# Pooling over shifted rows on the vector engine in place of a matrix product, in a two-block transformer kernel

## The reference, cut to what matters

```python
def centred_multiscale_pool(u):          # u (B, L, 4 groups, 512)
    cs = jnp.concatenate([jnp.zeros_like(uf[:, :1]), jnp.cumsum(uf, axis=1)], axis=1)
    left = win // 2                      # win = (2, 4, 8, 16), one for each group
    right = win - 1 - left
    hi = jnp.minimum(t + right + 1, L)
    lo = jnp.maximum(t - left, 0)
    s = cs[:, hi, g] - cs[:, lo, g]
    mean = s / (hi - lo)
    return (mean - uf)

def pool_branch(h, w_in, w_grp, b_grp, scale, w_out):
    u, gate = jnp.split(h @ w_in, 2, axis=-1)
    p = centred_multiscale_pool(u.reshape(B, L, 4, 512))
    p = jnp.einsum('blgc,gcd->blgd', p, w_grp) + b_grp
    y = p.reshape(B, L, 2048) * scale
    return (y * jax.nn.silu(gate)) @ w_out
```

## Time and profile before

| what | us |
|---|---|
| median of 3 runs | 2324.95 |
| lowest, highest | 2322.79, 2325.65 |
| the profiled execution | 2320.34 |
| its span | 2318.5 |
| TensorE busy | 2274.8 (98%) |
| DVE busy | 1677.5 (72%) |
| ACT busy | 1028.1 (44%) |

### The profile page before, as it was taken

How to read it: one execution, slowest core, us unless ns; L and a number is a source line. 1 busy time by engine, 2 the same in 40 slices (tenths; PEclk the granted TensorE clock), 3 DMA queues, 4 the chain that set the end, 5 groups by cost and what they waited for, 6 DMA issues and landing times.

```text
span 2318.5 us, 30884 instructions
## 1 busy us (share of the span) xinstructions
PE 2274.8 (98%) x11041; PEld 1885.8 (81%) x11041; DVE 1677.5 (72%) x2394; ACT 1028.1 (44%) x1474; POOL 77.9 (3%) x113
## 2 busy tenths in 40 slices
PE   8999999999999999999999999999999899999997
PEld 6878888888888888777878888888888799999876
DVE  5479976688788887787879676667874778666644
ACT  5565655555555554344462222222322634544432
POOL 1022200000000000000000000000000000000000
PEclk9999999999999999999999999999999999999999
DMA  8966645667676676787856555555664367422243
GB/s 243 215 185 207 192 137 172 196 215 229 213 238 223 223 228 204 232 264 245 258 169 211 170 180 162 174 156 164 227 200 132 121 188 219 132 74 63 72 158 133
DMA packets 225945, 430.33 MB, mean 186 GB/s; under 512 B 13847, under 2 KB 38671, under 8 KB 224688
## 3 DMA queue, kind: packets, MB, share of 16 engines
q1 hardware_dynamic: 222112, 418.96, 58.1%
q10 hardware_dynamic: 3152, 9.83, 1.3%
q0 software_dynamic: 576, 0.14, 0.0%
HBM read 426.16 MB, written 2.72 MB: 185 GB/s over the span
## 4 chain that ended last, share of the span: by engine, by line
PE 74%; issue 17%; DVE 4%; DMA 3%; ACT 1%; DVEq 0%; POOL 0%; SPq 0%; ACTq 0%; POOLq 0%
PE ps L641 46%; PE ps L676 13%; PE ps L653 10%; DMA raw<-in_w_down 2%; DVE ada_acc L610 1%; DVE lo L579 1%; PE ps L2437 1%; PE ps L2333 1%; PE ps L690 1%; ACT hi L575 1%; DMA xres<-in_x 1%; DMA raw<-in_w_up 0%; PE ps L2197 0%; PE ps L830 0%; DVE ustage L1794 0%
## 5 line engine op out<-in xcount | busy, mean ns | idle before, releaser
L575 ACT ACTIVATE hi<-raw 128x1024 fp32r<-128x1024 f32 x604 | 634.3, 1060 | 943.8 <-PE ps L641 358.1
L579 DVE TENSOR_TENSOR lo<-raw,hi 128x1024 fp32r<-128x1024 f32 x604 | 731.1, 1223 | 396.2 <-ACT hi L575 393.4
L610 DVE SCALAR_TENSOR_TENSOR ada_acc<-raw,csil,ada_acc 128x512 f32<-128x512 f32 x720 | 493.3, 749 | 4.8 <-DMA raw<-in_ada_w 4.6
L641 PE MATMUL ps<-hi,h_hi 128*128 128x512 f32 x960 | 382.1, 398 | 0.4 <-DVE lo L579 0.4
L641 PE MATMUL ps<-hi,h_lo 128*128 128x512 f32 x960 | 378.8, 395 | 0.0
L641 PE MATMUL ps<-lo,h_hi 128*128 128x512 f32 x960 | 378.8, 395 | 0.0
L641 PE MATMUL ps<-hi,g 128*128 128x512 f32 x704 | 227.2, 398 | 9.1 <-DVE lo L579 9.0
L641 PEld LDWEIGHTS ps<-hi,h_hi 128*128 128x128 f32 x960 | 180.8, 188 | 44.2 <-DVE lo L579 3.5
L641 PEld LDWEIGHTS ps<-hi,h_lo 128*128 128x128 f32 x960 | 180.7, 188 | 42.3
L641 PEld LDWEIGHTS ps<-lo,h_hi 128*128 128x128 f32 x960 | 180.9, 188 | 40.7
L641 PEld LDWEIGHTS ps<-hi,g 128*128 128x128 f32 x704 | 132.5, 188 | 44.2 <-DVE lo L579 14.2
(11 more groups left out here) (328 smaller groups left out, 3428.4 us busy)
## 6 DMA issues: line engine op xcount, KB each, us to landing
raw<-in_ada_w SPq DMA_DIRECT2D x192, 512.0 KB, 4.3
raw<-in_w_up SPq DMA_DIRECT2D x176, 512.0 KB, 4.5
raw<-in_w_down SPq DMA_DIRECT2D x88, 512.0 KB, 5.0
raw<-in_w_in SPq DMA_DIRECT2D x84, 512.0 KB, 4.6
raw<-in_pool_w_in SPq DMA_DIRECT2D x64, 512.0 KB, 4.4
raw<-in_mla_w_in SPq DMA_DIRECT2D x56, 448.0 KB, 4.1
raw<-in_w_out SPq DMA_DIRECT2D x32, 512.0 KB, 3.7
raw<-in_pool_w_out SPq DMA_DIRECT2D x32, 512.0 KB, 4.6
```

The lines of the kernel that those rows point to most:

```text
L575: act.activation(hi[:, to, :, :], raw[:, slot, :, :], ACT.Copy).then_inc(hi_split, 1 + ada)
L579: dve.tensor_tensor(lo[:, to, :, :], raw[:, slot, :, :], hi[:, to, :, :].bitcast(F32), ALU.subtract).then_inc(lo_split, 1)
L610: ins = dve.scalar_tensor_tensor(acc, raw[:, slot, k, :], csil[:, v, kt:kt + 1], acc, ALU.mult, ALU.add)
L641: mm = pe.matmul(ps[:, bank, 0:n], tokens(a, kt0 + k, tok), w[:, slot, k, col0:col0 + n], start=first and k == 0 and s == 0, stop=last and ...
```

## The change

What it does, on each engine:

- TensorE: the pooling product is gone. The u panel is made by `by_channels`, so that the weights are stationary and u comes out as channels by tokens. The product with `w_grp` moves from w12, w13 to w14, w15, behind six gate chunks (w8 to w13). w16 and w17 are the last two gate chunks. Both `turn_ada` now stand between w16 and w17. The u panel of groups 1 to 3 gets a wait for the first two silu of the group before (`gate_silu4`).
- ACT: copies u in two halves to `upad`, in which each row of 256 tokens has 8 zeros on either side. Rounds `pt_hi` from `upad`. Evicts the group product to `y` itself, with scale and bias.
- DVE: sums shifted rows (`window_sums`): level 0 adds the row and the row one token back, each further level adds two shifts of the level before, so that window 2^(n+1) takes n+1 additions, for each of two halves. An edge multiply corrects the first and last tokens. Then `upad = sums / window - upad`, and `pt_lo` from it. The eviction of y is gone.
- the banks: in group 0 the u panel is in banks 0, 1, 6, 7 and the gate in 2 to 5, and the norms of the stage ahead move their banks to fit. The first panel's parts for context and latent tokens are 256 columns wide on 24 weight tiles, in place of 512 columns on 12 token tiles.
- ACT no longer loads `poolm` in the w_down stage (four loads of 256 KB), but one small table `edges`.

```diff
+    edges = np.ones((POOL_G, 2, max(POOL_WINDOWS) // 2), np.float64)
...
+        def window_sums(e, n, half):
+            step = sums_done(n, half) - n - 2
+            spans = [(0, SEQ)]
+            for level in range(n, 0, -1):
+                spans.insert(0, (spans[0][0] - 2 ** (level - 1), spans[0][1] + 2 ** (level - 1)))
+            src = upad[:, 2 * half:2 * half + 2, :, :].rearrange("p m s t -> p (m s) t")
...
+            for level, (a, b) in enumerate(spans):
+                to = buffers[level % 2]
+                back, ahead = (1, 0) if level == 0 else (2 ** (level - 1), 2 ** (level - 1))
+                if level:
+                    e.wait_ge(window_summed, step + level)
+                e.tensor_tensor(to[:, :, reach + a:reach + b], src[:, :, reach + a - back:reach + b - back],
+                                src[:, :, reach + a + ahead:reach + b + ahead], ALU.add).then_inc(window_summed, 1)
...
# ACT
-                act.wait_ge(y_gated, FREE + n * 4)
-                act.activation(u[:, :, :], ps[:, 0:4, :], ACT.Copy).then_inc(u_ready, 1)
-                his(act, C_POOL, i, step, ahead(CH), ahead(CH + 2))
                 act.wait_ge(pt_lo_done, FREE + n)
+                for half in (1, 0):
+                    b0 = U_BANKS[n][2 * half]
+                    act.activation(upad[:, 2 * half:2 * half + 2, :, reach:reach + SEQ],
+                                   ps[:, b0:b0 + 2, :].rearrange("p m (s t) -> p m s t", s=2), ACT.Copy).then_inc(u_ready, 1)
+                his(act, C_POOL, i, step, ahead(CH), ahead(CH + 4))
...
+                his(act, C_POOL, i, step, ahead(CH + 4), ahead(CH + 8))
+                act.wait_ge(chunks_used, done(CH + 7))
+                for m in range(4):
+                    ins = act.activation(y[:, n * 4 + m, :], ps[:, U_BANKS[n][m], :], ACT.Identity,
+                                         scale=col(V_POOL_S, n * 4 + m), bias=col(V_POOL_B, n * 4 + m))
+                ins.then_inc(grouped, 1)
                 if n == POOL_G - 1:
...
+                    his(act, C_POOL, i, step, ahead(CH + 8), ahead(CH + 9))
                     for k in range(Y_FIRST):
                         y_high(k)
# DVE
-                split(place_of(0) + RING, place_of(CH + 2) + RING)
+                split(place_of(0) + RING, place_of(CH) + RING)
+                dve.wait_ge(u_ready, 2 * n + 2)
+                sums = itertools.chain(window_sums(dve, n, 0), window_sums(dve, n, 1))
+                for k in range(3):
+                    for _ in itertools.islice(sums, -(-2 * (n + 2) // 3)):
+                        pass
+                    split(place_of(CH + k) + RING, place_of(CH + k + 1) + RING)
...
-                ins.then_inc(grouped, 1)
# TensorE
+                    pe.wait_ge(gate_silu4, (n - 1) * 4 + 2)
+                    for j in range(CH):
+                        by_channels(pe, i * step + at, split_slot(at), h4_hi, h4_lo, CK_T * j, U_BANKS[n], j == 0, j == CH - 1, ada_behind(at))
...
-                            mm = pe.matmul(ps[:, m, s * SEQ + c0:(s + 1) * SEQ], u[:, TT * (1 - s) + k, m * P:(m + 1) * P],
-                                           poolm[:, bass.ds(n, 1), k, c0:].rearrange("p a b -> p (a b)"),
...
+                for j in range(6):
+                    chunk(j, h4_hi, h4_lo, CK_T * j, GATE_BANKS[n], j == 0, False)
+                pe.wait_ge(u_ready, 2 * n + 2)
                 pe.wait_ge(pt_lo_done, FREE + n + 1)
+                for j in range(6, 8):
+                    chunk(j, pt_hi, pt_lo, CK_T * (j - 6), U_BANKS[n], j == 6, j == 7)
+                for j in range(8, 10):
+                    if j == 9:
                         pe.wait_ge(grouped, FREE + n + 1)
...
                         turn_ada(pe, ada0, 0, 0)
+                        turn_ada(pe, ada0 + 1, 1, U_BANKS[n][2])
```

More of the change, by code:

```diff
@@ L443, in two_block_kernel @@
         h4_lo = pl("h4_lo", [P, KT, NT * P], F32R)
-        u = pl("u", [P, NT, W])
+        reach = max(POOL_WINDOWS) // 2
+        padded = SEQ + 2 * reach
+        window_at = pl.at
+        windows = [[pl("windows_first", [P, 4, padded]), None], [pl("windows_second", [P, 4, padded]), None]]
+        gsilu = [Place(window_at + 2 * KIB * m)(f"gsilu{m}", [P, W])[:, :] for m in range(2)]
         pt_hi = pl("pt_hi", [P, 4, NT * P], F32R)
         pt_lo = pl("pt_lo", [P, 4, NT * P], F32R)
-        poolm = pl("poolm", [P, POOL_G, TT, SEQ])
-        gsilu = [u[:, m, :] for m in range(2)]
+        windows[1][1] = Place(pl.at - 4 * 4 * padded)("windows_second2", [P, 4, padded])
+        upad = pl("upad", [P, 4, 2, padded])
+        edges = pl("edges", [P, POOL_G, 2, reach])
+        windows_first2 = [at(8 * n)(f"windows_first2_{n}", [P, 4, padded]) for n in range(POOL_G)]
         shift_tmp = at(112)("shift_tmp", [P, SHIFT_BUFS, NT * P])
@@ L645, in by_tokens, with by_channels @@
             return mm
-        def by_channels(pe, c, slot, a_hi, a_lo, kt0, bank0, first, last, ada=0):
+        def by_channels(pe, c, slot, a_hi, a_lo, kt0, banks, first, last, ada=0, part=slice(0, NT * P), frees=True):
             pe.wait_ge(lo_split, c + RING + 1)
@@ L652, in by_channels @@
                     for s, (w, a) in enumerate(((hi, a_hi), (hi, a_lo), (lo, a_hi))):
-                        mm = pe.matmul(ps[:, bank0 + n, :], w[:, slot, k, n * P:(n + 1) * P], a[:, kt0 + k, :],
+                        mm = pe.matmul(ps[:, banks[n], part], w[:, slot, k, n * P:(n + 1) * P], a[:, kt0 + k, part],
                                        start=first and k == 0 and s == 0, stop=last and k == CK_T - 1 and s == 2)
-            mm.then_inc(chunks_used, 1 + ada)
+            if frees:
+                mm.then_inc(chunks_used, 1 + ada)
         def panel_by_tokens(pe, first, i, order, j0, a_hi, a_lo, outs, width, nk=KT, before=None):
@@ L1426, in _ @@
                     act.wait_ge(g_lo_done, FREE + N_UP)
-                    for g in range(POOL_G):
-                        act.dma_start(poolm[:, g, :, :], consts["pool"][:, g, :, :]).then_inc(poolm_loaded, 16)
-                        end = place(DOWN_ORDER, CTX_FROM + CH * g) + RING
-                        his(act, C_DOWN, i, step, at, end)
-                        at = end
-                        if g == 0:
-                            norm_squares(act, n_pool_ctx, lambda e, i: e.wait_ge(ctx_loaded, 16), 0, xn4[:, 0, :])
+                    act.dma_start(edges[:, :, :, :], consts["edges"]).then_inc(edges_loaded, 16)
+                    end = place(DOWN_ORDER, CTX_FROM) + RING
+                    his(act, C_DOWN, i, step, at, end)
+                    norm_squares(act, n_pool_ctx, lambda e, i: e.wait_ge(ctx_loaded, 16), 0, xn4[:, 0, :])
+                    at = end
                 his(act, C_DOWN, i, step, at, RING + step - int(last))
@@ L1888, in _ @@
                 split(end, mid)
-                take_ada(dve, i * 2 + ADA_DOWN, 5)
+                take_ada(dve, i * 2 + ADA_DOWN, 4)
                 at = mid
@@ new lines, in pool_group @@
+                for half in range(2):
+                    dve.wait_ge(window_summed, sums_done(n, half))
+                    v = upad[:, 2 * half:2 * half + 2, :, reach:reach + SEQ].rearrange("p m s t -> p (m s) t")
+                    dve.scalar_tensor_tensor(v, window_total(n, half)[:, :, reach:reach + SEQ], 1.0 / POOL_WINDOWS[n], v,
+                                             ALU.mult, ALU.subtract).then_inc(pooled, 1)
+                    if half == 0:
+                        split(place_of(CH + 3) + RING, place_of(CH + 4) + RING)
@@ L2386, in _ @@
                     panel_by_tokens(pe, C_DOWN, i, DOWN_ORDER, half * n, g_hi, g_lo, pair(half), W, FT, before=ada_before)
[L2387 removed]
             def first_pool_panel():
[L2391 to L2392 removed]
+                part = lambda s, j, frees: by_channels(pe, C_POOL + j, split_slot(C_POOL + j), h4_hi, h4_lo, CK_T * j, U_BANKS[0],
+                                                       s == CTX and j == 0, False, ada_behind(C_POOL + j),
+                                                       slice(s * SEQ, (s + 1) * SEQ), frees)
                 pe.wait_ge(ffn_added, PAIR + D // W - 1)
```

123 lines of the change are left out of this document (56 added, 67 removed).

## The result

The kernel after takes 2333.85 us (median of 7 runs, 2328.26 to 2338.24), the kernel before 2323.46 beside it (7 runs): a ratio of 1.0045, 95% interval 1.0031 to 1.0058. In a second job it was 2332.12 against 2321.13, 1.0048 (1.0032 to 1.0064). So the change costs 10 to 11 us. The range of 2317 to 2336 held the time. The likeliest case, no change, did not come: the kernel is slower.

The account below looks back on a forecast made before the run. TensorE, busy 2274.8 of 2318.5 us, was taken as the bound. Terms -21.2 + 7.8 + 8.8 + 6.9 + 0.5 - 1.1 = +1.7 gave 2322.0 us, or 2326.7 on the median; range 2317 to 2336.

Parts of the forecast that it names:

- The likeliest case, no change: Whole kernel: three new waits take the whole gain, +1.7 us, within the 4.6 us that count as no change; 52%.
- rival C: DVE's window sums: additions of shifted rows are slow, 1.6 us each, 9.3 over the forecast, 2336.0 us; 16%.
- The pooling product, -21.2: TensorE, all four groups: the product at L2437 goes, 4 x 5.31 us, all on the path.
- DVE's sums, 7.5 of waits without refills: TensorE waits for DVE's window sums, 5.1 us in group 3 and 2.4 in group 2; +7.8 with refills.
- The turns: Second ada turn waits for DVE's reduce of the first: 1.4 us in groups 0 to 2, 4.6 in group 3; +8.8.
- The silu: u panels 1 to 3 wait for two silu on ACT, 2.3 us each with a refill; +6.9 us.
- The first panel: First u panel: 24 products 256 wide per part in place of 12 of 512; +0.5 us for all.
- `poolm`'s loads, -1.1: w_down stage, where the chain runs over DMA: 256 KB less to load beside a weight saves 1.1 us.
- each new wait of TensorE costs its full length: Pooling stage: TensorE is always busy there, so every new wait adds its whole length to the time.
- 0.1 for a refill: TensorE: refilling the array after a wait was taken to cost 0.1 us each time.
- rival D: TensorE's clock falls after group 3's two long waits and group 2's: +4.2 us, 2330.9; 14%.
- Rivals A, B and C: A: DVE's sums cost nothing, 2318.9, 14%; B: no new TensorE wait, 2303.2, 4%; C: slow additions, 2336.0, 16%.

Follow-up runs that it names:

- x_before_fewer_products: Kernel before with the pooling product cut to the first of four products of each output, computing wrong values: 2309.37 us, ratio 0.9947.
- x_before_silu: Kernel before with only the wait for two silu of the group before added ahead of u panels 1 to 3: 2330.83 us, ratio 1.0052.
- x_both: Kernel after with the second turn's wait one reduce earlier and the silu wait kept in group 1 only: 2316.33 us, ratio 0.9978 to before.

## Why the prediction was wrong in its likeliest case

**What came true by luck:** the range held 2333.85, but its upper end stood there for rival C, slow additions, which did not come. The forecast's own range, 2322 to 2331, missed it.

**The pooling product, -21.2:** right. No L2437 is left, group 0 is 3.7 shorter (5.31 less one turn of 1.4 and small change), and x_before_fewer_products gives back what it removes.

**DVE's sums, 7.5 of waits without refills:** 6.8 measured, group 3 4.7 for 5.1, group 2 2.1 for 2.4, groups 0 and 1 none. Additions 1.28 for 1.22 to 1.28. A step that waits for the one before comes 1.31 after it, duration plus 0.03, where independent ones come at 1.14 (they are of 1024 elements; group 0's edge multiply comes 1.27 behind an addition of 1024). So the rule of the Trainium skill ("VectorE: DVE Perf Modes", "The DRAIN you can't avoid") that a semaphore costs nothing extra, measured there on copies, does not hold for these chains of additions. The wait came out between the 6.2 by that rule and the 7.5.

**The turns:** 1.32 three times and 4.52, for 1.3 and 4.5. **The silu:** 2.38 three times, for 2.2 before refills. **The first panel:** +0.3 for +0.5. Together the waits are 22.4 us, against 22.5 in the list of what would show it.

**`poolm`'s loads, -1.1:** not seen. Before the first changed product the second profile of after is 1.2 us later than before, no earlier. Whether 256 KB less to load is worth anything stays open, and the runs give the term no value.

**What failed is the step "each new wait of TensorE costs its full length"**, with 0.1 for a refill, and so the sum. The price beyond the length was left to rival D, and that had its size and its place wrong: it stood at 14% as "group 3's two long waits and group 2's", +4.2. The clock fell elsewhere and oftener. From the stretch rows: groups' TensorE time less the product is 391.89 before and 401.43 after, 9.5 us more. Some 2.4 of it are the ten starts behind the waits: one costs 0.22 to 0.27 where the products run at the full clock (1.09 for 0.87, 44.86 for 44.62), not the 0.1 of the sum, for which no row stood. The other 7 are products at the lower clock. With their starts, the u panels of groups 2 and 3 are 1.97 and 1.95 longer, the 72 products behind group 2's DVE wait 1.8 (18.52 for 16.74), group 3's second turn 1.1 (1.97 for 0.87) and its w17 0.7 (6.26 for 5.58), group 1's 408 products 0.6. The silu wait, priced at its length, has the most of it behind it, although it is only 2.38 us long; I had measured the price of a wait on one of 3.00 at the start of the kernel and taken length alone as the sign. Group 3's 3.29, the longest for DVE, brought none here (16.98). The forecast for the four groups was +2.3 with 1.0 for refills in it. Less that 1.0 and the 0.1 by which the waits were shorter, the 9.5 add 8.4, which gives the measured +10.7. The prediction said itself that no row of this stage has a wait of that length; with ten new waits in a stage that had none, 14% was too little.

**Rivals A, B and C** are out: the sums do cost, the waits are there, the additions run at 1.28. C's number, 2336.0, came near for another reason.

**What stays open:** why one wait of 2.4 us is followed by slow products and the next isn't (x_before_silu has both in one execution; group 1 of after has 0.6 us, in both profiles, and of x_both 1.8, behind the same wait). The runs show that it happens, not what decides.

## What to carry to other kernels

In a stage in which TensorE has never waited, a wait has a second price: here some of those of 2.1 to 4.5 us were followed by products at half the clock that cost up to 2 us more (those of 1.3 to 1.4 were not), and ten waits of 22.4 us together cost almost 32. So in such a stage price new waits at their length, and up to half of it again. Look at each wait for whether it is needed where it is written: two of the three here were needed in one group of four or not at all, and with them taken to that place, and one chunk reordered, +0.45% became -0.45%. And work moved to an engine with idle time helps only where the idle time can be reached: DVE idled 8 us ahead of the copy in groups 1 to 3, but it goes into the sums with only four chunks of the stream in hand, and neither new order of the ada chunks turned that time to use.
